# Conditioning vectors summed by dot products in the first feed-forward, gate chunks later, and re-spaced steps in the first mixer, in a two-block fp32 kernel

## The reference

```python
mod = silu(c) @ w_ada + b_ada                      # 9 x 1024
sh1, sc1, g1, sh2, sc2, g2, sh3, sc3, g3 = split(mod, 9)
h = h + 0.5 * g1 * swiglu(rmsnorm(h, norm_ff1) * (1 + sc1) + sh1, ff1)     # d_ff 2816
h = h + g2 * token_mixing(rmsnorm(h, norm_mix) * (1 + sc2) + sh2)
h = h + 0.5 * g3 * swiglu(rmsnorm(h, norm_ff2) * (1 + sc3) + sh3, ff2)
```

## Time and profile before

| what | value |
|---|---|
| three executions | 1681.01, 1681.07, 1685.11 us, median 1681.07 |
| span of the profiled execution | 1677.2 us |
| share of the span in which TensorE is busy | 90% (DVE 63%, ACT 43%, POOL 20%) |
| first feed-forward, first mixer, second feed-forward | 0 to 231, 231 to 466, 466 to 669 us of the span |
| second block's mixers and projections, then the experts | 669 to about 1020, then to 1677 us |

### The profile page before, as it was taken

The page is one execution under the profiler, slowest core; times in us unless marked ns, Lnnn a source line. Parts: engine busy times, 40 slices in busy tenths (PEclk is TensorE's granted clock), DMA queues, the critical chain, the costliest instruction groups (busy, mean ns, idle before and its releaser), DMA issues.

```text
span 1677.2 us, 21599 instructions
## 1 busy us (share of the span) xinstructions
PE 1515.3 (90%) x7972; PEld 1124.8 (67%) x7972; DVE 1056.0 (63%) x1930; ACT 720.5 (43%) x1581; POOL 335.0 (20%) x320
## 2 busy tenths in 40 slices
PE   6999989998989999899999997988978888888776
PEld 6899988898889998889996774544433444343222
DVE  5666675875665555668554155677777767677754
ACT  4444444344344544654342124434444444444443
POOL 0100010000010000100000013435444444444441
PEclk9999999999999999899999999999999999999999
DMA  8977756655555554333332649999999999999996
GB/s 331 343 245 271 250 187 219 225 197 191 189 183 189 180 184 151 113 114 101 101 101 101 251 171 363 373 419 421 422 421 421 421 421 422 422 421 421 421 421 256
DMA packets 91002, 463.67 MB, mean 276 GB/s; under 512 B 10768, under 2 KB 10928, under 8 KB 57872
## 3 DMA queue, kind: packets, MB, share of 16 engines
q0 software_dynamic: 39360, 277.58, 40.5%
q1 hardware_dynamic: 50688, 183.52, 31.7%
q10 hardware_dynamic: 848, 1.18, 0.2%
HBM read 460.15 MB, written 2.10 MB: 276 GB/s over the span
## 4 chain that ended last, share of the span: by engine, by line
PE 60%; DMA 21%; DVE 9%; ACT 7%; issue 2%; POOL 0%; SPq 0%; ACTq 0%; DVEq 0%; POOLq 0%
DMA Ft<-peer_uv,ids 14%; PE ps L1288 9%; PE ps L501 7%; PE ps L502 7%; PE ps L503 7%; DMA uhi<-peer_uv,ids 5%; PE ps L1109 3%; PE ps L626 2%; PE ps L627 2%; PE ps L628 2%; DVE Ft L2076 2%; PE ps L1191 2%; PE ps L545 2%; PE ps L547 2%; PE ps L546 2%
## 5 line engine op out<-in xcount | busy, mean ns | idle before, releaser
L1288 PE MATMUL ps<-Ft 128*128 128x512 f32 x792 | 383.6, 620 | 81.7 <-ACT Ft L2636 80.8
L1288 PEld LDWEIGHTS ps<-Ft 128*128 128x128 f32 x792 | 144.7, 194 | 298.1 <-ACT Ft L2636 166.4
L2076 DVE CUSTOM_DVE_ANT_0 Ft<-Ft 128x1024 f32<-128x1024 f32 x198 | 242.6, 1225 | 144.3 <-DMA Ft<-peer_uv,ids 135.4
L1313 DVE TENSOR_TENSOR wlo<-raw,whi 128x1024 fp32r<-128x1024 f32 x228 | 275.6, 1233 | 80.6 <-ACT whi L2100 80.1
L501 PE MATMUL ps<-uhi,whi 128*128 128x256 f32 x1088 | 314.9, 289 | 5.2 <-DVE wlo L1313 2.8
L502 PE MATMUL ps<-ulo,whi 128*128 128x256 f32 x1088 | 311.0, 286 | 0.0
L503 PE MATMUL ps<-uhi,wlo 128*128 128x256 f32 x1088 | 310.7, 286 | 0.0
L2756 POOL DMA_INDIRECT Ft<-peer_uv,ids x198 | 221.4, 1118 | 299.2 <-PE ps L1288 270.7
L2100 ACT ACTIVATE whi<-raw 128x1024 fp32r<-128x1024 f32 x228 | 229.9, 1048 | 17.5 <-PE ps L547 8.6
L501 PEld LDWEIGHTS ps<-uhi,whi 128*128 128x128 f32 x1088 | 212.2, 195 | 9.2 <-DVE ulo L1464 2.8
L502 PEld LDWEIGHTS ps<-ulo,whi 128*128 128x128 f32 x1088 | 212.1, 195 | 1.8 <-issue 0.5
(11 more groups left out here) (434 smaller groups left out, 2289.1 us busy)
## 6 DMA issues: line engine op xcount, KB each, us to landing
raw<-ff_gu SPq DMA_DIRECT2D x88, 512.0 KB, 4.8
raw<-w_ada SPq DMA_DIRECT2D x56, 512.0 KB, 4.8
raw<-ff_dn SPq DMA_DIRECT2D x44, 512.0 KB, 4.4
raw<-w_in SPq DMA_DIRECT2D x32, 512.0 KB, 3.6
raw<-w_in_s SPq DMA_DIRECT2D x28, 512.0 KB, 4.3
raw<-w_mod SPq DMA_DIRECT2D x16, 512.0 KB, 6.0
raw<-w_out SPq DMA_DIRECT2D x14, 512.0 KB, 4.4
raw<-w_in_m SPq DMA_DIRECT2D x12, 512.0 KB, 4.4
```

The costliest lines, as they stand in the source:

```text
L1288: ins = t.matmul(acc[r][c], diag[n % NDIAG], gbuf[SEAT[n]][:, 1024 + c * 512:1024 + (c + 1) * 512], start=False, stop=(n % 128 == 127))
L1313: v.tensor_tensor(lo, raw_slot(j), hi.bitcast(F32), ALU.subtract).then_inc(*up("lo", j))
L2076: v.tensor_tensor_reduce(pjunk, gbuf[SEAT[n]][:, 0:1024], xn[:, q // 8, :], 1.0, 0.0, ALU.mult, ALU.add, dots[:, n:n + 1]).then_inc(*up("d ...
```

## The change

It sorts the nine chunks into `GATES` (2, 5, 8), which stay as they were, and `MODS` (0, 1, 3, 4, 6, 7), all laid out by feature. Chunks 3, 4, 6 and 7 are now summed like 0 and 1: one `tensor_tensor_reduce` on VectorE for each of 32 blocks, all woven into the first feed-forward with gate chunk 2 (40 side items on 59 "w" items). Chunk 5 goes to the last eight "w" items of the mixer's projection, chunk 8 into the second feed-forward; the other 32 blocks of the projection have no side items. A chunk's sum is polled one item later than before. In the mixer the ticks begin with the parts of gv, four tiles earlier, and the steps of the generators are re-spaced on all three engines: one empty step behind the decay logits, one more in `moba`, silu(gog) at level 6, the head norm cut in two steps (`head_sums`, `head_scale`). GpSimd's `memset` moves ahead of the first residual. The diff, cut:

```diff
+def late(*chunks):
+    return [("mod", "w_mod", c, k) for c in chunks for k in range(8)]
+
+
+GATES = (2, 5, 8)
+MODS = (0, 1, 3, 4, 6, 7)
+
...
-    stream += weave(ff1[3:HELD - 22], ada(2, 3, 4)) + ff1[HELD - 22:]
+    stream += weave(ff1[3:HELD - 22], ada(2) + late(3, 4, 6, 7)) + ff1[HELD - 22:]
...
-    stream += weave(w1, ada(5, 6, 7, 8))
+    stream += w1[:32] + weave(w1[32:], ada(5))
...
-    stream += ffn_stream("ff2_gu", "ff2_dn")
+    ff2 = ffn_stream("ff2_gu", "ff2_dn")
+    stream += ff2[:6] + weave(ff2[6:36], ada(8)) + ff2[36:]
     return stream + weights("w_in2", 32) + weights("xa_wk", 8) + weights("xa_wv", 8)
...
         def ada_poll():
-            for c in range(2, 9):
-                if c in begun or not cur.done(ada_at[c, 7]):
+            for c in GATES:
+                if c in begun or not cur.done(ada_at[c, 7] + 1):
                     continue
                 begun.add(c)
...
-                if c % 3 != 2:
-                    for k in range(8):
-                        ins = t.matmul(o[:, k:k + 1], acc[:, k * 128:(k + 1) * 128], onescol,
-                                       start=True, stop=True)
-                else:
-                    for n in range(2):
-                        ins = t.matmul(o[:, n * 512:(n + 1) * 512], ones, acc[:, n * 512:(n + 1) * 512],
-                                       start=True, stop=True)
+                for n in range(2):
+                    ins = t.matmul(o[:, n * 512:(n + 1) * 512], ones, acc[:, n * 512:(n + 1) * 512],
...
             give("gla_lr", "gla_v", "la")
+            yield
             yield
             la3 = grid(gla_la, 2)
...
                 give(("gla_o", r), "gla_a", "o", r)
             yield
-            while "gog" not in st:
-                yield
+            yield
             yield
             yield
...
                 give(("moba_s", hh), "moba_v", "s", hh)
+            yield
             yield
             yield
...
-            st = set()
             ada_poll()
             ready = norm("mix", h)
             cols("gqk", 4, u, ready, "gqk", group=3)
             small_cols(0, "glr", ("glrT",))
-            rows("gv", 1, u, None, "gvc")
-            gens = [gla(st)]
+            gens = [gla()]
 
             def tick():
                 ada_poll()
                 step(gens)
+            rows("gv", 1, u, None, "gvc", tick)
             cols("mq", 4, u, None, "mqc", tick)
             cols("mk", 4, u, None, "mkc", tick)
             rows("mv", 1, u, None, "mvc", tick)
             gens.append(moba())
             rows("gog", 1, u, None, "gogc", tick)
-            st.add("gog")
             cols("gates", 16, u, None, "gatesc", tick)
             while gens:
...
+                elif stream[j][0] == "mod" and stream[j][2] > 1:
+                    late_sum(j, *stream[j][2:])
+
+        def late_sum(j, c, k):
+
+            s = mod_t[:, 8 * MODS.index(c) - 16:8 * MODS.index(c) - 8]
+            v.wait_ge(*at(f"raw{j % NRAW}", j))
+            if summed:
+                v.wait_ge(*at("ada", summed[-1]))
+            summed.append(j)
+            v.tensor_tensor_reduce(mod_v, raw_slot(j), crow, 1.0, 0.0, ALU.mult, ALU.add, s[:, k:k + 1]).then_inc(
+                *up("ada", j))
+            if k == 7:
+                v.wait_ge(*at("ada", j))
+                v.tensor_tensor(modc9[:, c, :], s, bcol9[:, c, :], ALU.add).then_inc(*up("mod", c, "sum"))
+                if c % 3 == 1:
+                    v.wait_ge(*at("mod", c, "sum"))
+                    v.scalar_tensor_tensor(gain3[:, c // 3, :], modc9[:, c, :], 1.0, vecs[:, (V_MIX, V_FF2)[c // 6], :],
+                                           ALU.add, ALU.mult).then_inc(*up("mod", c, "gain"))
...
+        def head_sums(key, o, n_heads, sqr, st, *ready):
...
+        def head_scale(key, o, n_heads, sqr, st, gate, dst):
...
+        def gla():
+            yield
             o = spot["gla_lr"]
             v.wait_ge(*at("gla_a", "ln"))
...
-            yield
-            while "gog" not in st:
-                yield
             g8 = grid(gog, 8)
             v.wait_ge(*at("gla_a", "gog"))
             v.wait_ge(*at("gn"))
             v.tensor_tensor(g8, g8, bc(gn.unsqueeze(1), [128, 8, 128]), ALU.mult).then_inc(*up("gla_v", "gog"))
+            yield
+            head_sums("gla", oa, 8, lev[0], hst_a, "gla_a", "o", 1)
+            yield
             v.wait_ge(*at("gla_v", "gog"))
-            head_norm("gla", oa, 8, lev[0], hst_a, gog, oa, "gla_a", "o", 1).then_inc(*up("gla_v", "out"))
+            head_scale("gla", oa, 8, lev[0], hst_a, gog, oa).then_inc(*up("gla_v", "out"))
             yield
             yield
...
             v.tensor_reduce(sm_b[:, 4:8], logit[:, :, 128:384], AX, ALU.max, negate=True).then_inc(*up("moba_v", "max"))
+            yield
             v.wait_ge(*at("moba_a", "e"))
...
             settle(a, a.activation(gla_e1, gla_e1, ACT.Exp, scale=-1.0), "gla_a", "exp")
+            yield
             a.activation(gla_e1, gla_e1, ACT.Ln, bias=1.0).then_inc(*up("gla_a", "ln"))
...
+                if lv == 6:
+                    a.wait_ge(*at("gogc", "gog", 0, 1))
+                    a.activation(gog, gog, ACT.Silu).then_inc(*up("gla_a", "gog"))
                 yield
             for r in range(2):
                 a.wait_ge(*at("gla_t", "o", r))
                 a.activation(oa[:, r * 512:(r + 1) * 512], spot["gla_o", r], ACT.Copy).then_inc(*up("gla_a", "o", r))
             yield
-            while "gog" not in st:
-                yield
-            a.wait_ge(*at("gogc", "gog", 0, 1))
-            a.activation(gog, gog, ACT.Silu).then_inc(*up("gla_a", "gog"))
+            yield
             yield
             yield
...
             ins.then_inc(*up("moba_a", "e"))
             yield
+            yield
...
         bias()
+        p.memset(att, 0.0).then_inc(*up("gla_p", "zero"))
         residual("ff1")
         p.wait_ge(*at("res", "ff1", 1, 1))
         row(("bg8",), G[2], D["b_ada"][8:9, :], 1024)
         row(("gn",), gn, D["gla_norm"], 128)
         power("mix")
-        p.memset(att, 0.0).then_inc(*up("gla_p", "zero"))
```

More of the change, by code:

```diff
@@ L1339, in ada_poll @@
                 v.wait_ge(*at("ada_t", c))
[L1340 to L1355 removed]
+                g = G[c // 3]
+                v.wait_ge(*at(f"bg{c}"))
+                v.tensor_tensor(g, o, g, ALU.add).then_inc(*up("mod", c, "sum"))
+                if c != 5:
+                    v.wait_ge(*at("mod", c, "sum"))
+                    v.tensor_scalar(g, g, 0.5, None, ALU.mult).then_inc(*up("mod", c, "half"))
         def mean_square(name):
@@ L1574, in both_norms, with heads, head_norm, gla @@
             norm_low("mem", vecs[:, V_MEM, :], 1, m[1], m[0])
-        def head_norm(key, o, n_heads, sqr, st, gate, dst, *ready):
+        def heads(x):
+            return x.rearrange("p (h d) -> p h d", d=128)
+        def head_sums(key, o, n_heads, sqr, st, *ready):
             n = n_heads * 128
-            x3 = lambda x: x.rearrange("p (h d) -> p h d", d=128)
-            a, c = (st[:, k * n_heads:(k + 1) * n_heads] for k in (1, 2))
             v.wait_ge(*at(*ready))
             settle(v, v.tensor_tensor(sqr[:, 0:n], o, o, ALU.mult), "hn", key, "sq")
-            settle(v, v.tensor_reduce(st[:, 0:n_heads], x3(sqr[:, 0:n]), AX, ALU.add), "hn", key, "sum")
-            v.tensor_scalar(a, st[:, 0:n_heads], 1.0 / 128, EPS, ALU.mult, ALU.add).then_inc(*up("hn", key, "ms"))
+            settle(v, v.tensor_reduce(st[:, 0:n_heads], heads(sqr[:, 0:n]), AX, ALU.add), "hn", key, "sum")
+            v.tensor_scalar(st[:, n_heads:2 * n_heads], st[:, 0:n_heads], 1.0 / 128, EPS, ALU.mult,
+                            ALU.add).then_inc(*up("hn", key, "ms"))
+        def head_scale(key, o, n_heads, sqr, st, gate, dst):
+            n, c = n_heads * 128, st[:, 2 * n_heads:3 * n_heads]
             v.wait_ge(*at("hnp", key))
-            settle(v, v.tensor_tensor(x3(sqr[:, 0:n]), x3(o), bc(c.unsqueeze(2), [128, n_heads, 128]), ALU.mult),
+            settle(v, v.tensor_tensor(heads(sqr[:, 0:n]), heads(o), bc(c.unsqueeze(2), [128, n_heads, 128]), ALU.mult),
                    "hn", key, "x")
             return v.tensor_tensor(dst, sqr[:, 0:n], gate, ALU.mult)
-        def gla(st):
+        def head_norm(key, o, n_heads, sqr, st, gate, dst, *ready):
+            head_sums(key, o, n_heads, sqr, st, *ready)
+            return head_scale(key, o, n_heads, sqr, st, gate, dst)
+        def gla():
+            yield
             o = spot["gla_lr"]
@@ L1666, in block1_mix @@
             cols(4, group=3)
-            rows(1)
-            gens = [gla(st)]
+            gens = [gla()]
             def tick():
@@ L1672, in tick @@
                 step(gens)
+            rows(1, after=tick)
             cols(8, after=tick)
@@ L2333, in to_cols @@
                 return lambda i, j: copy(dst(i), spot[name, i][:, 0:256], j, name + "c", name, i)
-            rows(1, to_rows(grid(gv, 2), "gv"))
-            gens = [gla(st)]
```

(4 more changed lines are left out.)

34 lines of the change are left out of this document (9 added, 25 removed).

## The result

The changed kernel takes 1665.22 us (median of 4 executions, 1664.43 to 1666.80) where the kernel before, run beside it, takes 1683.09 (1681.01 to 1686.43): a ratio of 0.9898, 95% interval 0.9880 to 0.9916. Of 1681 us that is 17.1 us less (14 to 20). The forecast was 21.35 us less, 1659.7: the saving is 4.2 us smaller, the time itself 5.5 us above, and inside its range. A second profile of each kernel was taken with the experiments; the changed kernel then gave 1665.46 us, ratio 0.9901 (0.9880 to 0.9922). One execution of `gate_last` (2473 us) and two of the kernel before beside it (3001 and 3174 us) were in a slow state, and no ratio counts them.

The account below looks back on a forecast made before the run. TensorE, busy for 90% of the span, was taken to bound the kernel. Gains 6.8 + 3.6 + 0.55 + 3.0 - 1.0 + 8.4 = 21.35 us gave 1659.7 us against 1681.07; range 1653 to 1669 us.

Parts of the forecast that it names:

- four column sums off TensorE: Shift and scale chunks: eight one-column matmuls each, 1.68 us, four chunks on the path; gain 6.8 us.
- chunk 6's stop and slow stretch: Mixer, L466: TensorE's 1.9 us stop for the accumulator and 1.7 of low clock behind it go; gain 3.6 us.
- memset: Mixer norm: the first scaled identity no longer runs beside GpSimd's memset; gain 0.55 us, range 0 to 0.7.
- decay logits: Mixer, L704: the 2.3 us stop shrinks to 1.1, gain 1.3, and no slow stretch behind it, 1.7 more.
- moba: Mixer: L792's 1.9 us stop goes, about 2.8 at gates tile 2 comes, slow stretch as today; net 1.0 us lost.
- head norm: Mixer, L772: the stop of 5.4 us and its 3.0 of slow clock go; gain 8.4 us.
- 16 side items in the first feed-forward, loads: First feed-forward: VectorE's extra items covered by TensorE's 8.5 us a step, loads at 310 GB/s; cost taken as 0.
- the third rival: Opening: weave begins when loads are crowded, a late ScalarE split passes on 1 to 4 us; 1661 to 1664 us, chance 0.13.
- moba's split did come late: Mixer, gates tile 2: the rival denied this lateness, so 2.8 + 1.7 us go too; 1655.2 us, chance 0.12.
- the spacing was not a tick short: Mixer waits: the rival claimed spacing one tick short, 4 to 8 us less gain; 1664 to 1668 us, chance 0.17.
- the stage was not bound by its loads: First feed-forward: the rival claimed it becomes load-bound, slower below 280 GB/s; 1695 us, chance 0.05.
- the sums are no relief: Mixer: stops of the same length move to other steps, time stays within 0.3%; chance 0.04.

Follow-up runs that it names:

- gate_last: The changed kernel with gate chunk 2 woven behind chunks 3, 4, 6 and 7 instead of ahead of them: 1666.41 us, ratio 0.9898.
- late_weave: The changed kernel with the 40 side items woven from the first feed-forward's twelfth weight on instead of the third: 1664.63 us, ratio 0.9894.
- early_end: The changed kernel with the first feed-forward's last side item twelve weights before the stage's end instead of four: 1664.74 us, ratio 0.9898.
- late_early: The changed kernel with the 40 side items woven between the twelfth weight and the twelfth from the end: 1664.28 us, ratio 0.9893.
- memset_back: The changed kernel with GpSimd's memset at its old place behind the row of gn: 1667.34 us, one execution.
- gate_last_late_exp: The changed kernel with chunk 2 last in the weave, the weave starting at the twelfth weight, moba's exponentials in two halves: 1663.13 us, ratio 0.9876.
- shift_67: The changed kernel with the sums of chunks 6 and 7 moved from the first feed-forward into the mixer: 1666.03 us, ratio 0.9903.
- sums_only: The changed kernel with the mixer generators' ticks and steps as in the kernel before, the rest of the change kept: 1680.29 us, ratio 0.9991.

## Why the forecast was right, and where it was 4 us off

| step of the prediction | forecast, us | two profiles and runs, us |
|---|---|---|
| four column sums off TensorE | 6.8 | the mixer's two: with chunk 8's sum moved out, its rest is 5.9 less; the feed-forward's two: rest 2.3 less, stops more |
| chunk 6's stop and slow stretch | 3.6 | stop gone |
| memset | 0.55 | 0.53 |
| decay logits | 3.0 | stop 2.3 to 0.8, clock not low |
| moba | -1.0 | stop at L792 of 1.9 gone, 2.5 at gates tile 2; no slow stretch in two profiles |
| head norm | 8.4 | stop 5.4 gone, clock not low |
| 16 side items in the first feed-forward, loads | 0 | stops 2.2 and 3.3 us more, although the memset takes 0.5 off them |

**The mixer** went by its steps. Stops: forecast 1.9 + 1.3 - 0.9 + 5.4 = 7.7 us less, measured 8.3 to 8.7. Clock: forecast 6.4 less, measured 8.0, because the slow stretch that I left behind moba didn't come in either profile of the changed kernel. With the same stop it did come in `late_weave`, `early_end`, `late_early`, `gate_last` and `memset_back`, so that part of the step was right for this spacing, and what it takes is chance. The sum of chunk 8 (L470) only moved, as said: the mixer's rest shrinks by 5.9 us, 2.5 beyond the 3.4 of the two sums, and the second feed-forward's grows by 2.2.

Beside the memset the scaled identities took three times as long, and do so again when it is put back; at its new place it costs nothing that the profiles show. By the rule of the Trainium skill (SBUF — State Buffer, "Who interferes with whom") that was to be expected, and the trace agrees. Its other half, that a subtraction with two SBUF inputs is held up by GpSimd instructions that read, shows too: in the kernel before, at the end of the mixer, four subtractions take 6.61 us beside GpSimd's two additions of the residual, the first two 1.95 and 2.32 us each where one otherwise takes 1.22, and in every other profile the first two are as slow.

```profile
455.37 3.54 POOL L2698 TENSOR_TENSOR Ft<-Ft 128x512 f32<-128x512 f32 x2 [65.16 <-DVE Ft L1439]
455.81 6.61 DVE L1313 TENSOR_TENSOR wlo<-raw,whi 128x1024 fp32r<-128x1024 f32 x4
```

The stop for the decay logits is 0.82 us in every kernel with the new spacing, 0.3 less than the 1.1 that the rows had given. The drain behind a table load (Trainium skill, ScalarE: Activation LUTs, "What ACT_TABLE_LOAD costs") would by that page's figures have left about 3.9 us, an estimate; the measurement speaks against it here.

**What failed** is the first step: "there are four such chunks, each on the path. Gain 4 x 1.7". For the two in the first feed-forward it doesn't hold. That stage with the memset was to be 3.95 us shorter and is 1.9 longer, 5.8 off: stops 3.3 of it (2.75 us more instead of 0.55 less), clock 1.35, rest 1.15 (2.25 us less instead of 3.4). The mixer is 2.8 us better than forecast (clock 1.6, stops 0.8, rest 0.35), opening, second block and experts 1.2 worse: 5.8 - 2.8 + 1.2 = 4.2, the whole error.

I had looked at whether VectorE and the loads keep up inside a step, and they do: from 62 to 220 us TensorE never stops for more than 0.4 us, at 305 and 309 GB/s in the two profiles, where 310 was forecast. I had not looked at what runs beside each sum that goes. The one of chunk 4 filled a hole of 1.52 us, so there the gain was 1.84 - 1.52 = 0.3 us. This rests on comparing kernels with and without the sum; no run put a column sum back alone. VectorE's last dot product with its additions, and in one profile a late load, add 0.5 to 0.9 (1.99, and 2.03 + 0.36, against 1.52). The stop at 58 us adds 0.7 to 1.8. That last one is the third rival's mechanism, a late split in the crowded opening, and its size; it came beside the forecast, not in its place. A stop is there in all seven profiles of kernels with 40 side items woven from the third weight on, 0.38 us in `gate_last`, 0.5 to 1.8 in the others. None is there where the weave starts at the twelfth weight (`late_weave`, `late_early`, `gate_last_late_exp`), nor with 24 side items (`shift_67`). So it comes from side items packed into the opening; why it is so much longer in one profile than in another stays open. What the clock took in this stage can't be put down to the change: the kernel before lost 0.0 us to it once and 3.4 the other time.

One sign that the prediction had named as wrong did come, a granted clock below 1.00 inside 60 to 220 us; it came in the second profile of the kernel before as well, so it doesn't speak against the change. ScalarE's waits for `raw` between 60 and 220 us, the other sign, sum to 7.9 us in the changed kernel, none over 1.2; TensorE stopped for at most 0.4 us in that time, from 62 us on.

The range held. Of the rivals, moba's split did come late, the spacing was not a tick short, and the stage was not bound by its loads: they carried 372 GB/s where that rival needed them to fail at 280. That the sums are no relief is wrong as well, though with the old spacing alone it was nearly right (`sums_only`). Second feed-forward and experts were costed at nothing; apart from the sum of chunk 8 (2.2 us into the former, as much out of the mixer) the profiles show nothing there that can be told from chance.

## What to carry to other kernels

Before you credit an instruction's removal with its own duration, look at what the other engines do during it: if a chain of theirs ends just behind it, the instruction was filling a hole, and its removal gives only the part that the hole doesn't take back. The same holds for a stop: taken away alone, it uncovers the next late chain (here moba's exponentials). When what a change to a schedule gives is a few microseconds in 1665, judge them by stops and work stage by stage in two profiles, since the clock alone moves a stage by 3 us from one execution to the next of the same kernel.

## What the runs showed of the hardware

A stretch of low clock does not need a stop just ahead of it: in the kernel before, once more, TensorE was granted 0.77 from 55 to 70 us while it was busy for 15.00 of 15 us, and the first profile of the same kernel has no low stretch there. Of the fourteen profiles eleven have one that begins at 58 to 62 us, with stops of 0 to 1.8 us ahead; in all fourteen TensorE has just run bucket products (L588, L593) or is still at them, from 55 to 56.5 us on. The other way round, the stop of 2.5 us at gates tile 2 was followed by none in both profiles of the changed kernel and by one of 3.4 us in five relatives. So a single slow stretch can't be booked on a single stop from one profile.

The loads ran at 372 GB/s over 50 us beside a TensorE that never stopped (`late_early`), against 256 in this stage in the kernel before, 310 in the changed kernel and 333 in `late_weave`.
